# Query weights kept in the ring: tile 0's heads projected alone in plain fp32, tile 1's between tile 0's expert rows

## The reference, cut to what matters

```
q = (hb @ peer_wq).reshape(B, Q_BLOCK, PEER_HEADS, 2, PEER_HALF)      # 8 heads x 2 x 128
s = einsum('bqhpd,hpnd->bqhpn', q, peer_subkeys)                      # 128 keys per half
vals, idx = top_k(s, 16)                                              # 16 of each half
combo = vals[..., 0, :, None] + vals[..., 1, None, :]                 # 256 pairs
ids = idx[..., 0, :, None] * 128 + idx[..., 1, None, :]
top_s, pos = top_k(combo, 16)                                         # 16 experts per head
expert = take_along_axis(ids, pos);  g = softmax(top_s)
a = gelu(einsum('bqhkd,bqd->bqhk', peer_u[expert], hb))
out = einsum('bqhk,bqhkd->bqd', g * a, peer_v[expert])
```

## Time and profile before

| | |
|---|---|
| median of 3 executions | 1795.46 us (1793.21 to 1800.6) |
| the profiled execution | 1796.3 us, span 1794.5, mean granted TensorE clock 0.968 |
| TensorE busy | 1645.6 us, 92% |
| VectorE, ScalarE, GpSimd busy | 1121.9, 651.9, 457.5 us |
| DMA | 542.70 MB, 302 GB/s over the span; expert rows 269.50 MB |

### The profile page before, as it was taken

How to read it: one execution, slowest core, us unless ns; L and a number is a source line. 1 busy time by engine, 2 the same in 40 slices (tenths; PEclk the granted TensorE clock), 3 DMA queues, 4 the chain that set the end, 5 groups by cost and what they waited for, 6 DMA issues and landing times.

```text
span 1794.5 us, 29256 instructions
## 1 busy us (share of the span) xinstructions
PE 1645.6 (92%) x11820; PEld 1489.0 (83%) x11820; DVE 1121.9 (63%) x1897; ACT 651.9 (36%) x1235; POOL 457.5 (25%) x343
## 2 busy tenths in 40 slices
PE   5998996879988799999995999999999999999997
PEld 3986785879878789999994748998999896989997
DVE  3685378676676587887877762225557448665554
ACT  4544443322223244343102114525444531344442
POOL 0663453445444434444343320000000000000000
PEclk8999998989989999999997999999999999999999
DMA  9469687999999999999998988876355540545442
GB/s 375 170 237 390 272 327 318 399 419 409 412 416 419 420 370 421 421 416 421 420 419 351 394 358 367 347 295 263 114 187 189 187 183 1 188 165 212 174 161 89
DMA packets 58306, 542.70 MB, mean 302 GB/s; under 512 B 6464, under 2 KB 6592, under 8 KB 7744
## 3 DMA queue, kind: packets, MB, share of 16 engines
q1 hardware_dynamic: 21168, 271.37, 38.3%
q0 software_dynamic: 37008, 269.50, 36.7%
HBM read 539.80 MB, written 1.05 MB: 301 GB/s over the span
## 4 chain that ended last, share of the span: by engine, by line
PE 69%; DMA 13%; DVE 10%; issue 4%; ACT 2%; POOL 1%; SPq 0%; POOLq 0%; DVEq 0%; ACTq 0%
PE psum L467 69%; DMA arena<-in_experts,idx_stage 9%; DMA ring<-in_w_ada 2%; DVE arena L2107 1%; DVE arena L2096 1%; POOL arena L1144 1%; DMA ring<-in_w_ffn 1%; DMA ring<-in_w_out 1%; DMA ring<-in_peer_wq 1%; DVE small L2000 0%; DVE arena_r L1714 0%; DVE arena L1953 0%; DVE ring_r L1648 0%; DVE small L1951 0%; DVE x_t L2025 0%
## 5 line engine op out<-in xcount | busy, mean ns | idle before, releaser
L2096 DVE CUSTOM_DVE_ANT_0 arena<-arena 128x1024 f32<-128x1024 f32 x256 | 313.7, 1226 | 160.4 <-DMA arena<-in_experts,idx_stage 154.9
L1144 POOL DMA_INDIRECT arena<-in_experts,idx_stage x256 | 307.7, 1202 | 342.7 <-DVE arena L2107 154.6
L1648 DVE TENSOR_TENSOR ring_r<-ring,ring_r 128x1024 fp32r<-128x1024 f32 (+1 forms) x172 | 207.2, 1212 | 186.5 <-ACT ring_r L1187 185.7
L467 PE MATMUL psum<-small,arena 128*128 128x128 f32 x2080 | 259.0, 288 | 64.3 <-ACT small L1522 63.4
L467 PEld LDWEIGHTS psum<-small,arena 128*128 128x128 f32 x2080 | 253.4, 203 | 70.3 <-ACT small L1522 53.0
L467 PE MATMUL psum<-small_r,ring_r 128*128 128x256 f32 x1600 | 286.6, 282 | 4.1 <-DVE h_t_r L1735 4.1
L467 PE MATMUL psum<-h_t,ring 128*128 128x256 f32 (+1 forms) x1552 | 269.3, 335 | 16.7 <-ACT h_t L1449 14.0
L467 PEld LDWEIGHTS psum<-h_t,ring 128*128 128x128 f32 x1552 | 241.0, 192 | 42.2 <-ACT h_t L1449 14.4
L467 PE MATMUL psum<-arena_r,ring_r 128*128 128x256 f32 x1680 | 266.3, 284 | 1.3 <-DVE arena_r L1714 1.3
L467 PEld LDWEIGHTS psum<-small_r,ring_r 128*128 128x128 f32 x1600 | 246.2, 189 | 6.1 <-issue 5.8
L1187 ACT ACTIVATE ring_r<-ring 128x1024 fp32r<-128x1024 f32 (+1 forms) x172 | 178.9, 1047 | 165.2 <-PE psum L467 151.2
(11 more groups left out here) (256 smaller groups left out, 1605.9 us busy)
## 6 DMA issues: line engine op xcount, KB each, us to landing
ring<-in_w_ffn SPq DMA_DIRECT2D x35, 2048.0 KB, 8.8
ring<-in_w_in SPq DMA_DIRECT2D x31, 2048.0 KB, 8.9
ring<-in_w_ada SPq DMA_DIRECT2D x27, 2048.0 KB, 10.2
ring<-in_w_ffn SPq DMA_DIRECT2D x24, 1408.0 KB
ring<-in_w_out SPq DMA_DIRECT2D x4, 2048.0 KB
ring<-in_peer_wq SPq DMA_DIRECT2D x4, 2048.0 KB, 9.9
ring<-in_p_ret SPq DMA_DIRECT2D x4, 2048.0 KB
arena<-in_w_ada SPq DMA_DIRECT2D x3, 2048.0 KB, 11.9
```

Of the source, the lines that this page charges most:

```text
L467: return nc.tensor.matmul(o, a, b, start=first, stop=last)
L1144: nc.gpsimd.indirect_dma_start(rows[slot % GBUF], None, dram["experts"], bass.IndirectOffsetOnAxis(ap=idx_stage[:, slot:slot + 1], axis=0) ...
L1648: nc.vector.tensor_tensor(whole(i, ring_r), whole(i, ring), upper(i).bitcast(F32), ALU.subtract).then_inc(lo_made, 1)
L2096: step(nc.vector.tensor_tensor_reduce(u, u, h2[:, n // PER_TILE, :], 1.0, 0.0, ALU.mult, ALU.add, dots[:, n % 8, s:s + 1]), sem("dots"))
```

## The change

- *Order of weights.* Mods 4 to 21 all come before the query; between the slabs of `w_in` stand 1, 2, 2, 2, 2, 2 of them instead of 0, 0, 0, 2, 0, 2. The four slabs of `peer_wq` come last and fill the ring's four slots. `SPARE` and its slab are gone.
- *h.* `n2` makes plain h: DVE scales, ACT shifts (`h_whole`), no high and low part. `peer_wq` is not split.
- *Query.* `query(t, i)` multiplies slab i with one tile's 128 tokens in plain fp32 (32 matmuls), into three turning buffers `pq_t`. Before the rows PE does `query(0, 0)`, the turns of h of tile 0, `ks0_0`, then `query(0, 1)` to `query(0, 3)` with `ks0_1`, `ks0_2`. Tile 1's are 19 chunks (`second_query`) ahead of the context's in the same generator: 8 in batch 0, then one a batch to batch 11; each of its slabs is released behind its last chunk. The context's 13 chunks begin at batch 24.
- *Choice.* Identities of tile 0 go out for each of the four blocks. Eight steps (block 0, three of block 1) stand before the first dot; the other 34 of both tiles are spread over 56 batches. Tile 0's gates are made for each block, with an exponential on ACT for each.
- *Buffers.* The row buffers are free from before h is shifted. `subkeys` moves to `arena[0:2048]`, so SP loads it behind `w_out`'s last split piece, and the context is gathered behind the first list of 32 rows and `ks1_3`.

```diff
-SPARE, GAP = 21, 22
+GAP = 22
@@
-CTX_FIRST, CTX_SECOND = 5 + 4 * ALONE, 127 - 4 * ALONE
+QUERY_FIRST, QUERY = 8, 19
+CTX_START = 24
+CTX_FIRST, CTX_SECOND = QUERY + 5 + 4 * ALONE, 127 - 4 * ALONE
 CTX_LAST = PER_TILE - 3
+BLOCK_STEPS = 5
+CHOICE_FIRST, CHOICE = BLOCK_STEPS + 3, 2 * (BLOCK_STEPS * PH // 2 + 1)
@@ slab_order
-    first = (mods[:4] + w_in(0) + [("w_idx", 0, KD * 136)] + w_in(1) + w_in(2) + w_in(3) + mods[4:6] + w_in(4) + w_in(5)
-             + mods[6:8] + w_in(6) + mods[8:13] + out_proj + mods[13:15] + peer(0) + mods[15:17] + peer(1)
-             + mods[17:19] + peer(2) + mods[19:21] + peer(3))
+    first = (mods[:4] + w_in(0) + [("w_idx", 0, KD * 136)] + mods[4:5] + w_in(1) + mods[5:7] + w_in(2) + mods[7:9] + w_in(3)
+             + mods[9:11] + w_in(4) + mods[11:13] + w_in(5) + mods[13:15] + w_in(6) + mods[15:20] + out_proj + mods[20:22])
+    first += [slab for i in range(4) for slab in peer(i)]
@@
 def context_due(n):
+    if n < CTX_START:
+        return min(QUERY_FIRST + n, QUERY)
     if n < PER_TILE:
-        return min(n + 1, PER_TILE - 4) * CTX_FIRST // (PER_TILE - 4)
+        return QUERY + min(n + 1 - CTX_START, PER_TILE - 4 - CTX_START) * (CTX_FIRST - QUERY) // (PER_TILE - 4 - CTX_START)
@@
 def choice_due(n):
-    return max(n - 3, 0) * 2 // 5
+    return min(CHOICE_FIRST + (n + 1) * (CHOICE - CHOICE_FIRST) // (PER_TILE - 8), CHOICE)
+
+def choice_made(step):
+    return next(n for n in range(PER_TILE) if choice_due(n) >= step)
@@
-        published = [[PH // 4, PH // 2], [PH // 2]]
+        published = [list(range(1, PH // 2 + 1)), [PH // 2]]
@@ tensor (the mod_steps between the projections follow the new order)
+            def query(t, i):
+
+                w = query_slab(i)
+                o = begin(f"pq{t}_{i}", "act")
...
+                for n, (j, k) in enumerate(order):
+                    if t == i == j == 0:
+                        pe.wait_ge(sem("h_whole"), KD + k + 1)
+                    last = mm(o[:, j * P:(j + 1) * P], w[:, k, j * P:(j + 1) * P], h_t[:, k, t * P:(t + 1) * P],
+                              n == 0 or by_head and k == 0, n == 4 * KD - 1 or by_head and k == KD - 1)
+                    if t and n % KD == KD - 1:
+                        if j == 3:
+                            ctx_end(f"pq{t}_{i}", last)
+                            release(n=peer[i][1])
+                        yield
+                if t == 0:
                     end(last)
...
+            for _ in query(0, 0):
+                pass
+            turn_h(0)
+            pe.wait_ge(sem("subkeys"), 16)
+            key_scores(0, 0)
+            mod_steps(GAP, GAP)
+            for i in (1, 2, 3):
+                for _ in query(0, i):
+                    pass
+                if i > 1:
+                    key_scores(0, i - 1)
@@
+            def second_query():
+
+                yield from query(1, 0)
+                key_scores(0, 3)
+                yield from query(1, 1)
+                key_scores(1, 0)
+                yield from query(1, 2)
+                key_scores(1, 1)
+                yield from query(1, 3)
+                key_scores(1, 2)
+                yield
+                turn_h(1)
+                yield
+                key_scores(1, 3)
+                yield
@@ sync
-                if slabs[n][:2] == ("peer_wq", 1):
-
-                    sp.wait_ge(sem("y_mix"), 2 * KA)
+                if slabs[n][:2] == ("peer_wq", 2):
+
+                    sp.wait_ge(*piece_read[first_pieces - 1])
                     sp.dma_start(subkeys.rearrange("p h n -> p (h n)"), dram["subkeys"][0]).then_inc(sem("subkeys"), 16)
@@ gpsimd
-            pool.wait_ge(sem("lane"), 1)
-            pool.wait_ge(*slab_free[slabs.index(("peer_wq", 3, SLAB))])
...
             for known, (t, r0, r1) in enumerate(lists):
+                if known == 1:
+
+                    pool.wait_ge(sem("lane"), 1)
+                    pool.wait_ge(group_done, index["ks1_3"] + 1)
+                    nc.gpsimd.indirect_dma_start(ctx_t.rearrange("p k t -> p (k t)"), None, dram["ctx"],
@@ scalar
+            norm_hi("n2", None, None, [f"wo{i}" for i in range(4)], sq1, between={KD: lambda: mod_steps(20, 21, False)})
             act.sem_inc(sem("row_free_pe"), GBUF)
             act.sem_inc(sem("row_free_dve"), GBUF)
+            mod_steps(21, 22, False)
+            for k in range(KD):
+                act.wait_ge(sem("n2_scaled"), k + 1)
+                nc.scalar.activation(h_t[:, k, :], h_t[:, k, :], ACT.Identity,
+                                     bias=mod1[:, 24 + k:25 + k]).then_inc(sem("h_whole"), 1)
@@
             for n in range(BATCHES):
                 if n == 0:
                     best_exp(0)
+                for g in range(1, PH // 2):
+                    if n == choice_made(BLOCK_STEPS * (g + 1)) + 1:
+                        best_exp(0, g)
@@ vector
+            while choices < CHOICE_FIRST:
+                next(chosen)
+                choices += 1
+            v.wait_ge(*emptied("ht0_1"))
             dot_batch(0)
```

More of the change, by code:

```diff
@@ L194, in program @@
     slots, last_in_split = slots_of(slabs, ctx_at, tail_at, second_at)
-    split = [n for n in range(len(slabs)) if (n >= second_at or slabs[n][0] in ("w_in", "w_out", "peer_wq"))
+    split = [n for n in range(len(slabs)) if (n >= second_at or slabs[n][0] in ("w_in", "w_out"))
              and slabs[n][0] != "w_ada_2"]
@@ L199, in program @@
     first_out = sum(slabs[p[0]][0] == "w_in" for p in pieces)
-    first_peer = first_out + sum(slabs[p[0]][0] == "w_out" for p in pieces)
     first_pieces = sum(p[0] < second_at for p in pieces)
```

202 lines of the change are left out of this document (108 added, 94 removed).

## The result

The changed kernel took **1819.27 us** (median of 4, 1817.65 to 1821.64), the kernel before 1797.95 beside it; the ratio is 1.0116, 95% interval [1.0098, 1.0135]. It is slower, by 21 us, where 1780 had been forecast, and it lies above the range of 1767 to 1802. The profiled execution took 1817.65 us, with a span of 1815.9.

The account below looks back on a forecast made before the run. PE was taken to bound the first part and the end, DMA tile 0's rows. First gather -35.5, moved bytes +14.7, load +5: -15.8 from the profiled 1796.3, so 1780.5, as a median 1780 us; range 1767 to 1802.

Parts of the forecast that it names:

- What bounds the kernel, and the block from tile 0's end on: PE bounds the first part, DMA tile 0's rows; from those rows' end nothing changes, 1156 us to the end.
- The front, +14.5: Up to the root of n2: seven more modulation slabs and turns on PE move it from 202.75 to 217.2.
- Stepping the order through: Front: with 11.4 us of PE for a w_in slab, each slab lands before its reader; w_in 6 nearest to late.
- if PE waits for slabs between 60 and 165 us: Front: named, with PE bursts leaving DMA idle in batches 0 to 12, as what would above all make it wrong.
- rival 1: PE's 46 us idle from 302 to 640 is latency, not slack; with a front 8 us worse: 1788, 22%.
- Norm to first gather, 33.6: From the root of n2 at 217.2, through query and choice, to the first gather at 250.8, 35.5 us earlier.
- Bytes, +14.7: Full-rate stretch: 6.1 MB of context slabs and context gather come behind the first gather, 14.7 us at 0.414.
- Load, +5 (0 to 13): Tile 0's rows: fuller engines lower the DMA rate; 13 us if all ran at 400 GB/s, 5 taken.
- 2, the loop becomes the bound: Row buffers' loop, with choice steps and query chunks, loses 10% in each of 56 batches, +31 us: 1806, 15%.
- its sign (380): Mean rate from first gather to tile 0's last row: 380 GB/s shows rival 2, where 405 to 414 was forecast.
- rival 3: Gathers issued slowly, up to 1.90 us each, load term goes to 13: 1788, 5%; its sign is 400 GB/s.
- 4, more gain than summed: No load term, w_out wait gone (-3), query at full clock (-2): -26 in all, 1770, 8%.

Follow-up runs that it names:

- e2_small: Changed kernel with modulation slabs 4 to 14 loaded to one eighth, same instructions, their true values left out: 1794.0 us, ratio 0.9974.
- e11_ctxsmall: Changed kernel with the first three context slabs loaded to one eighth, 5.5 MB less: 1810.6 us, ratio 1.0060.
- e3_explate: Changed kernel with ACT's exponentials of blocks 1 to 3 behind their batch's diagonals, gates of blocks 1 and 2 one top16 later: 1808.2 us, ratio 1.0054.
- e7_exp3: Changed kernel with exponentials of blocks 1 to 3 three batches after the block's last choice step, not one, and gates one top16 later: 1809.1 us, ratio 1.0064.
- e9_mid: Changed kernel with modulation slabs spread evenly, exponentials of blocks 1 to 3 three batches late, PSUM bank rotation set to the changed kernel's: 1797.3 us, ratio 0.9983.
- e15_midonly: Changed kernel with e9_mid's even slab order and bank rotation, exponentials left as in the changed kernel: 1810.0 us, ratio 1.0060.
- e14_lump: e13_ctxroot with DVE's index work of a head block cut in two, six steps a block instead of five: 1789.3 us, ratio 0.9960.
- e13_ctxroot: e9_mid with ACT's square root of the first context norm, and what follows it there, one batch later: 1796.8 us, ratio 0.9988.
- e5_oldorder: Changed kernel with the earlier kernel's order among the w_in slabs, then modulation slabs 8 to 19 in one run: 1832.4 us, ratio 1.0191.
- e8_smallexp3: Changed kernel with the edits of e2_small and e7_exp3 together: 1792.1 us, ratio 0.9955.
- e16_after_again: The changed kernel itself, run again on the chip of e13_ctxroot, e14_lump and e15_midonly: 1817.0 us, ratio 1.0109.
- e6_single: Changed kernel with one modulation slab, not two, between most w_in slabs: 1825.1 us, ratio 1.0138.

## Why the prediction was wrong

- *What bounds the kernel, and the block from tile 0's end on.* Right: 1157.6 us against 1158.5, counted from the issue of the 136th gather. (One line was read loosely: DMA's nines stand in slices 8 to 21 and 23 of the earlier trace rows, the rest to 26 are 8s, and slice 7 is a 7. No sum uses it.)
- *The front, +14.5.* PE's work was summed right: 14.4 us more, and e2_small's root stands at 217.3. The step that failed is "Stepping the order through [...] each slab lands before its reader". I had given each slab its own transfer time and compared the mean rate with what DMA can do (319 against 414 GB/s). What counts is when a slab can be issued and what is in the queue with it. A `w_in` slab is issued 3.6 us behind its pair, has the pair's bytes to wait for and needs 14.9 us to land, where it needs 7.5 to 8.5 behind a pair of small ones; PE runs dry before it is landed and split. That is 15 us of idle PE, and 8 more by the lower clock that came with it. A mean over the stretch says nothing on that. The text named this as what would make it wrong, "if PE waits for slabs between 60 and 165 us", and priced it at 8 us within rival 1; it was 23.
- *Norm to first gather, 33.6.* 30.7. Query and choice came as costed or a little better, and the cast stood at its fast value, with POOL idle beside it, where it had been 2.25 us beside POOL's split:

```profile
269.62 0.18 DVE L2086 CAST ids<-small 128x32 uint32<-128x32 f32 x1
...
271.33 1.12 POOL L1193 DMA_INDIRECT arena<-in_experts,idx_stage  x1 [0.98 <-POOL idx_stage L1186]
```

  The rule of the Trainium skill ("SBUF — State Buffer", Who interferes with whom) that DVE and POOL wait for each other at a shared port pair agrees with this.
- *Bytes, +14.7.* 6.8 MB more passed in the stretch than before (150.0 MB over 386.9 us at 388 GB/s, against 143.2 over 349.6 at 409; 136 gathers each). e11_ctxsmall gives them about half to two thirds of full price while there are holes. The term is of the right kind; it is not larger than I said.
- *Load, +5 (0 to 13).* This is the second failure: with the bytes at full price (6.8 / 0.409 = 17 us) 20 of the 37.3 us to the 136th gather are left. I had priced load as a lower mean rate from full engines. Outside the holes the rate was full (417 and 418 GB/s, and in 400 to 420 PE was busy 7.6 us only). The loss was waits of one engine in its own order: an exponential that waits for the end of DVE's index work, with the next batch's diagonals behind it. I listed ACT's four exponentials by duration and table load (2.6 us each) and did not ask what each waits for; for `gates(0, 0)` I did, for blocks 1 to 3 not. The runs price it: 9 to 13 us for ACT's place in line (e3_explate, e7_exp3, e9_mid against e15_midonly), and 7.5 for the undivided index work and the places of the steps once that was out of the way.
- *Rivals.* 1, idle time as latency: not it; shorter waits shortened the run. 2, the loop becomes the bound: it had the right side, 1806, and DVE's step ahead of the dot is part of the truth, but not as 10% in every batch. The mean rate, 388 GB/s, stands between its sign (380) and that of rival 3 (400), so the sign alone would have misled. 3: gather issues had a median of 0.94 us in the stretch against 0.96; not it. 4, more gain than summed: no.
- *What holds of the change itself.* Its idea, gathers behind a short path from the norm, gave 52.9 us from root to first gather (83.6 to 30.7). It paid 37.9 in front of it and 35.6 behind. Other orders of issue give back 12 of the first (the four traces with that front have roots of 228.6 to 232.7, and e14_lump's is the earliest) and 24 of the second (e14_lump; 21 counted to the 136th gather, since its 129th comes 9.6 us behind its 128th). The rest of the first is PE's work for seven more slabs, 14.6, and 11 to 15 us of landings (idle PE and its lower clock) that no order tried here has hidden.

## What to carry to other kernels

With a ring of few slots, step through the order by issue times: when is the slot free, what else is in the queue at that moment, and how much work has the reader until it has landed. A mean rate hides it, and a different order may only move the wait, so try an even one. When an instruction is put into an engine's order, ask what it waits for and what stands behind it, not what it lasts; then ask again for the next one, since one such repair here (e13_ctxroot) gave nothing by itself; whether it has a part in what e14_lump gave, no run tells.

## What the runs showed of the hardware

- A slab of 2.1 MB issued 3.6 us behind two others of its size landed 14.5 to 14.9 us after its issue (in one case 5.4 MB moved meanwhile, at 364 GB/s); behind two of one eighth it landed in 7.5 to 8.5 us (e2_small).
- In some traces ACT stood for 10.8 to 12.4 us right behind the first gathers, released by nothing that the profile knows:

```profile
269.94 0.60 ACT L1265 ACTIVATE arena<-psum 128x512 f32<-128x512 f32 x1 [0.30 <-PE psum L475]
282.89 1.09 ACT L1265 ACTIVATE arena<-psum 128x512 f32<-128x512 f32 x2 [12.35 <-remote]
```

It was there in the changed kernel and in all four runs of the set e5_oldorder to e8_smallexp3, in none of the other twelve, which ran on other chips; e16_after_again is the same kernel without it, 2.3 us faster at the median. So it goes with the set or its chip and not with the kernel. That it is ACT's instructions being fetched behind the eight gathers' packets is only a guess; nothing here was made to test it, and the packets of instructions in the traces don't settle it (in e5_oldorder and e6_single one of 16 KB comes 1.5 to 2 us before ACT goes on, in the other three the next comes 5 us after).
- PE's granted clock was 0.66 as a mean over the 20 us (660 to 680, e5_oldorder) in which it stood 10.3 us for a PSUM bank, and 1.00 in the same 20 us without that wait.
